# Hybrid conv/HGRN2/MoE layer on one core: the output half of a tile follows its own recurrence by two tiles instead of by a block of four

## What is computed

```python
h = rms_norm(x, g_pre_mix) * (1.0 + sc1) + sh1
cv, cg, q, f, i, g = jnp.split(h @ w_in, IN_SPLITS, axis=-1)
y_conv = conv_module(cv, cg, dw_kernel, dw_bias, conv_ln_gain, conv_ln_bias)  # GLU, 31 taps, LayerNorm, swish
y_rec = hgrn2(q, f, i, g, lb_table, rec_norm_gain)   # chunks of 64, 4 heads, per-head RMSNorm, output gate
y = jnp.concatenate([y_conv, y_rec], axis=-1) @ w_out
x = x + gt1 * rms_norm(y, g_post_mix)
h = rms_norm(x, g_pre_ffn) * (1.0 + sc2) + sh2       # router, then top-2 of 32 SwiGLU experts
x = x + gt2 * rms_norm(hier_moe(h, ...), g_post_ffn)
```

## Time and profile before

| | us |
|---|---|
| median of 3 runs | 1842.37 (1840.76 to 1842.48) |
| the profiled execution | 1839.05 |
| its span, first to last instruction | 1837.5 |
| `project` of blocks 1, 2, 3 | 135.3, 135.4, 135.5 |
| `steps` of blocks 0, 1, 2, 3 | 126.9, 127.2, 127.3, 120.1 |
| tail of the mixer | 75.0 |
| routing and experts | 626.9 |

### The profile page before, as it was taken

One profiled execution on the slowest core, in us unless ns is written; L12 is line 12 of the kernel. 1 busy time (PEld: TensorE's weight loads), 2 busy tenths in 40 slices (PEclk: granted clock), 3 DMA queues, 4 the chain that ended last, 5 costly groups with the idle time before them and its releaser, 6 DMA issues. The chain is left out here.

```text
span 1837.5 us, 24383 instructions
## 1 busy us (share of the span) xinstructions
PE 1533.9 (83%) x7268; PEld 1152.0 (63%) x7270; DVE 1296.4 (71%) x1999; ACT 841.1 (46%) x1443; POOL 374.0 (20%) x403
## 2 busy tenths in 40 slices
PE   2597945699998899998899998926989999999960
PEld 2486824488855789666689475425667666666730
DVE  5489966679965499865599652257667877778738
ACT  1422232433363522454322542313767787878745
POOL 1000000000010000010000010114546666665640
PEclk9999966799998899998899998956989999999985
DMA  9255114133322232322331122372999998889948
GB/s 341 76 157 187 52 43 163 64 94 107 98 81 71 81 110 73 92 92 92 84 100 47 38 89 81 126 237 82 314 338 301 302 341 263 241 229 315 279 97 363
DMA packets 200424, 291.29 MB, mean 159 GB/s; under 512 B 10558, under 2 KB 158171, under 8 KB 200346
## 3 DMA queue, kind: packets, MB, share of 16 engines
q1 hardware_dynamic: 169762, 193.03, 31.4%
q0 software_dynamic: 30416, 97.19, 18.9%
q10 hardware_dynamic: 168, 0.06, 0.0%
HBM read 240.42 MB, written 59.26 MB: 163 GB/s over the span
## 5 line engine op out<-in xcount | busy, mean ns | idle before, releaser
L892 DVE SCALAR_TENSOR_TENSOR cv<-u,taps,cv 128x512 f32<-128x512 f32 x480 | 321.7, 743 | 0.6 <-DVE yT L848 0.3
L1741 DVE TENSOR_TENSOR w_rest<-wgu,w_high 128x1024 fp32r<-128x1024 f32 x192 | 233.7, 1221 | 94.5 <-ACT w_high L1666 93.3
L1666 ACT ACTIVATE w_high<-wgu 128x1024 fp32r x192 | 201.5, 1054 | 139.3 <-PE pgu L1616 86.0
L416 PE MATMUL bank<-hT_high,tiles_operand 128*128 128x512 f32 x512 | 204.6, 400 | 35.7 <-DVE hT_operand L866 21.1
L417 PE MATMUL bank<-hT_operand,tiles_operand 128*128 128x512 f32 x512 | 203.2, 397 | 0.0
L418 PE MATMUL bank<-hT_high,win_operand 128*128 128x512 f32 x512 | 202.9, 396 | 0.0
L439 PE MATMUL bank<-wo,yT 128*128 128x512 f32 x432 | 189.7, 594 | 0.0
L1626 PE MATMUL py<-wd,hTe 128*128 x384 | 172.6, 592 | 0.9 <-ACT yb L1693 0.9
L1614 PE MATMUL pgu<-w_high,x_high 128*128 128x512 f32 x384 | 155.3, 404 | 0.0
L1616 PE MATMUL pgu<-w_high,x_rest 128*128 128x512 f32 x384 | 151.0, 393 | 0.0
L1615 PE MATMUL pgu<-w_rest,x_high 128*128 128x512 f32 x384 | 151.0, 393 | 0.0
(11 more groups left out here) (345 smaller groups left out, 2910.4 us busy)
## 6 DMA issues: line engine op xcount, KB each, us to landing
win<-w_in_in SPq DMA_DIRECT2D x64, 512.0 KB, 5.2
wgu<-w_gate_in SPq DMA_DIRECT2D x32, 1024.0 KB
wgu<-w_up_in SPq DMA_DIRECT2D x32, 1024.0 KB
wd<-w_down_in SPq DMA_DIRECT2D x32, 1024.0 KB
wo<-w_ada_in POOLq DMA_DIRECT2D x8, 2048.0 KB, 9.2
win<-w_in_in SPq DMA_DIRECT2D x16, 1024.0 KB, 5.2
y_dram<-zeros POOLq DMA_DIRECT2D x17, 512.0 KB, 5.3
win<-x_in SPq DMA_DIRECT2D x16, 512.0 KB, 4.5
```

What stands on the lines that cost most here:

```text
L416: nc.tensor.matmul(out[:], high[:, k, cols], hT_high[:, k, :], start=(k == 0), stop=False)
L892: ins = V.scalar_tensor_tensor(out=cv[:, j], in0=u[:, j, w:w + T], scalar=tap, in1=cv[:, j], op0=ALU.mult, op1=ALU.add)
L1666: A(w_high[:, QK * q:QK * q + QK, :], c.wgu[:, bass.ds(slot, 1), QK * q:QK * q + QK, :].rearrange("p a k n -> p (a k) n"), ACT.Copy).then_ ...
L1741: V.tensor_tensor(w_rest[:, part, :], c.wgu[:, bass.ds(slot, 1), part, :].rearrange("p a k n -> p (a k) n"), w_high[:, part, :].bitcast(F3 ...
```

## The change

- The unit of delay is the tile. In `steps(t)` the output half is done for four tiles w = 0 to 3 that are numbers 4t-2+w (`tile_no`): the last two tiles of block t-1, and the **first two of block t itself**. Thus `steps(0)` gets two tiles of it, the steps of blocks 1 to 3 four each as before, and the tail has two instead of four.
- For that, a tile's outputs are normed, gated, turned and saved by themselves: `orstd` and `gateo` and `oT` for each i, in the order of the lists. The outputs of tiles 2 and 3 are turned in the next block's `project`, behind its first piece. `yT` holds two tiles instead of a block, so `place` copies one tile at a time, when the `y` two tiles before has been done.
- All three lists are new. TensorE turns the tiles of block t+1 (`T` 0, `T` 1) right behind `B` 1 and ahead of `O` 1; `T` 2 and `T` 3 ahead of `O` 3; the lists end with `O` 3, `r` 3, `l` 2 and `l` 3.
- `centre`, `sq` and the first `ysum` move into `heads`, between the heads' exponentials.
- `win_high` gets a third buffer, so a piece may be rounded when the piece three before has been used. The added slot is free memory for `xsum` and for two tiles of `last_modulation`.
- In block 0 the products of w_ada's fifth vector move from VectorE (`ada_sums(4)`) to TensorE (`ada_products(4)`, 64 matmuls with one column behind `mean`). Its pieces 10 and 11 can be loaded only behind those products, and w_out behind `ada_sums(5)`, which VectorE does at `scale` and `mask` 0. `last_modulation` comes behind `B` 1 on TensorE and `osave` 0 on VectorE instead of behind `O` 3.

```diff
-        tiles, win_high = overlaid("tiles", [P, 2, 2 * D])
+        tiles, win_high = overlaid("tiles", [P, NSLOT, 2 * D])
...
-        yT = sb("yT", [P, KD, T])
+        yT = sb("yT", [P, 2, KD, P])
...
-        STEPS = [("y", 0, 0), ("mean",), ("y", 0, 1), ("y", 1, 0), ("var",), ("A", 0), ("y", 1, 1), ("B", 0), ("r", 0), ("O", 0),
...
+        tile_no = lambda t, w: t * NT - 2 + w
+        STEPS = [("y", 0, 0), ("mean",), ("y", 0, 1), ("var",), ("y", 1, 0), ("A", 0), ("y", 1, 1), ("B", 0), ("r", 0), ("A", 1), ("O", 0),
+                 ("l", 0), ("B", 1), ("T", 0), ("T", 1), ("O", 1), ("r", 1), ("A", 2), ("oT", 0), ("l", 1),
+                 ("y", 2, 0), ("B", 2), ("y", 2, 1), ("oT", 1), ("O", 2), ("y", 3, 0), ("y", 3, 1),
+                 ("A", 3), ("r", 2), ("B", 3), ("T", 2), ("T", 3), ("O", 3), ("r", 3), ("l", 2), ("l", 3)]
+        TAIL = [("y", 0, 0), ("y", 0, 1), ("y", 1, 0), ("y", 1, 1), ("r", 0), ("l", 0), ("r", 1), ("l", 1)]
...
+                if not isinstance(t, int) or t < NB:
+                    wait_apart(pool, proj_ready, (t + 1) * AU, pool_passed)
...
+            store(0, (2, 3))
+            with pool.Fori(1, NB) as t:
+                store(t, (0, 1, 2, 3))
+            store(NB, (0, 1))
...
+            def ada_products(m):
+                for half in range(2):
+                    p = 2 * m + half
+                    pe.wait_ge(*ada_load(p))
+                    for j in range(KD):
+                        for k in range(4):
+                            last = nc.tensor.matmul(bank[3][:, m * KD + j:m * KD + j + 1], ada_slot[slot_of(p)][:, k, j * P:(j + 1) * P],
+                                                    cond[:, 4 * half + k:4 * half + k + 1], start=(half == 0 and j == 0 and k == 0),
+                                                    stop=(half == 1 and k == 3), skip_group_check=True)
+                    last.then_inc(ada_used, 1)
+                pe.wait_ge(ada_used, 2)
+                pe.sem_inc(ada_cols_done, 1)
             def ada_columns(m):
...
+                    if j == 0 and not with_ada:
+                        turn_outputs(t - 1, 2)
+                        turn_outputs(t - 1, 3)
+            def y_half(t, w, half, take):
+                if half == 0:
                     pe.wait_ge(wo_in, 16)
-                    pe.wait_ge(yT_rec, (t + 1) * NT)
-                    pe.wait_ge(yT_conv, (t + 1) * NCH)
-                out = next(banks)
+                    pe.wait_ge(yT_rec, tile_no(t, w) + 1)
+                    pe.wait_ge(yT_conv, tile_no(t, w) + 1)
+                out = take(("y", w, half))
                 for k in range(KD):
...
+                if i >= 2:
+                    pe.wait_ge(yT_rec, t * NT + i - 1)
...
             def turn_outputs(t, i):
+                pe.wait_ge(o_gated, t * NT + i + 1)
                 if i == 0:
-                    pe.wait_ge(o_gated, t + 1)
-                if i >= 2:
-                    pe.wait_ge(yT_rec, t * NT + i - 1)
+                    pe.wait_ge(keT_ready, t * NT + 3)
+                else:
+                    pe.wait_ge(state_ready, t * 2 * NT + (5 if i == 1 else 2 * NT))
...
+            steps(0, 2, True, {("mean",): lambda: ada_products(4), ("B", 1): last_modulation})
...
-                if j >= 2:
-                    act.wait_ge(proj_ready, t * AU + 2 * (j - 2) + 2)
-                elif before is not None and j == 0:
-                    act.wait_ge(logit_ready, (before + 1) * NT)
-                    for s in range(2):
-                        act.wait_ge(x1_stored[s], (before + 1) * 32)
-                        act.wait_ge(xn_stored[s], (before + 1) * 32)
-                A(win_high[:, j % 2], win[:, j % NSLOT], ACT.Copy).then_inc(high_ready, 1)
...
+                if j >= NSLOT:
+                    act.wait_ge(proj_ready, t * AU + 2 * (j - NSLOT) + 2)
+                elif isinstance(before, int) and before == 0 and j == 0:
+                    act.wait_ge(row_done, 2)
+                elif before is not None and j == 1:
+                    act.wait_ge(logit_ready, tile_no(before, 3) + 1)
+                    for s in x1_stored:
+                        act.wait_ge(s, 32 * before + 16)
+                elif before is not None and j == 2:
+                    for s in xn_stored:
+                        act.wait_ge(s, 32 * before + 16)
...
+                    if j == 0 and before is not None:
+                        save_turned(before, 2)
+                        save_turned(before, 3)
...
+                    if h == 0:
+                        squares(t)
...
+                    if h == 2 and first == 0:
+                        y_sums(t, 0, place_of(STEPS))
...
-            ORDER = [("sq",), ("ysum", 0), ("var",), ("key", 0), ("x1sum", 0), ("ysum", 1), ("rin", 0), ("osq", 0), ("key", 1),
...
+            ORDER = [("var",), ("x1sum", 0), ("key", 0), ("gate",), ("ysum", 1), ("rin", 0), ("key", 1), ("osq", 0), ("orstd", 0),
+                     ("x1sum", 1), ("xsum", 0), ("xsum", 1), ("osq", 1), ("orstd", 1), ("T", 0), ("T", 1), ("rin", 1),
+                     ("key", 2), ("turned", 0), ("xsum", 2), ("xsum", 3), ("ysum", 2), ("turned", 1), ("osq", 2), ("orstd", 2),
+                     ("x1sum", 2), ("key", 3), ("ysum", 3), ("rin", 2), ("T", 2), ("T", 3), ("split", 0), ("x1sum", 3),
+                     ("osq", 3), ("orstd", 3), ("rin", 3), ("split", 1)]
...
+                centre(t)
...
-            def gate_outputs(t):
-                dve.wait_ge(o_rstd, t + 1)
-                o3 = ob[:].rearrange("p i (h n) -> p (i h) n", h=NH)
-                V.tensor_tensor(o3, o3, sums[:, 32:48].unsqueeze(2).to_broadcast([P, NT * NH, P]), ALU.mult).then_inc(v_rec, 1)
-                dve.wait_ge(v_rec, t + 1)
-                dve.wait_ge(g_done, t + 1)
-                V.tensor_tensor(ob[:], ob[:], gs[:], ALU.mult).then_inc(o_gated, 1)
...
+            def gate_outputs(t, i):
+                dve.wait_ge(o_rstd, t * NT + i + 1)
+                for h in range(NH):
+                    hc = slice(h * P, (h + 1) * P)
+                    last = V.scalar_tensor_tensor(out=ob[:, i, hc], in0=ob[:, i, hc], scalar=sums[:, 32 + 4 * i + h:33 + 4 * i + h],
+                                                  in1=gs[:, i, hc], op0=ALU.mult, op1=ALU.mult)
...
-            ORDER = [("centre",), ("ynorm", 0), ("scale",), ("mask", 0), ("x1norm", 0), ("state", 0), ("ynorm", 1), ("osave", 0), ("oms", 0),
...
+            ORDER = [("ynorm", 0), ("scale",), ("mask", 0), ("x1norm", 0), ("state", 0), ("ynorm", 1), ("osave", 0), ("mask", 1), ("conv",),
+                     ("oms", 0), ("place", 0), ("x1norm", 1), ("state", 1), ("gateo", 0), ("logit", 0), ("xnorm", 0), ("xnorm", 1), ("osave", 1),
+                     ("T", 0), ("T", 1), ("oms", 1), ("mask", 2), ("logit", 1), ("gateo", 1), ("place", 1), ("input", 0), ("input", 1),
+                     ("state", 2), ("xnorm", 2), ("xnorm", 3), ("osave", 2), ("ynorm", 2), ("oms", 2), ("x1norm", 2), ("mask", 3), ("gateo", 2),
+                     ("ynorm", 3), ("state", 3), ("place", 2), ("T", 2), ("T", 3), ("input", 2), ("input", 3), ("osave", 3), ("x1norm", 3),
+                     ("piece", 0), ("oms", 3), ("logit", 2), ("gateo", 3), ("place", 3), ("logit", 3), ("piece", 1)]
...
+            steps(0, 2, True, {("scale",): lambda: ada_sums(5, (0,)), ("mask", 0): lambda: ada_sums(5, (1,)),
+                               ("osave", 0): last_modulation})
...
```

More of the change, by code:

```diff
@@ L1075, in steps @@
+            TAIL_ORDER = [("ynorm", 0), ("x1norm", 0), ("ynorm", 1), ("x1norm", 1), ("logit", 0), ("logit", 1)]
+            def steps(t, first, nxt, after={}):
+                places = place_of(STEPS)
+                for step in ORDER:
+                    kind, *at = step
                     if kind in ("ynorm", "x1norm", "logit"):
-                        if out:
+                        if at[0] >= first:
                             if kind == "x1norm":
-                                x1_norm(t - 1, *at)
+                                x1_norm(t, *at)
```

448 lines of the change are left out of this document (236 added, 212 removed), and 5 rows, old and new, of the table STEPS.

## The result

The changed kernel takes 1874.3 us (median of 4 runs, 1870.16 to 1878.05); the kernel before took 1841.98 beside it. The ratio is 1.0178 (95% interval 1.0157 to 1.0199): slower by 32 us, where 21 were forecast. The profiled execution took 1870.16 us for a span of 1868.6, which is 31.1 more than before.

A forecast was written before the change was run, and what follows sets the result against it. TensorE's idle time in the steps, set by the order of three lists, was taken as the bound. 27.7 + 27.4 - 0.7 - 33.4 = +21.0 on the median 1842.37 gave 1863 us; forecast 1847 to 1877, range with rival 3 1840 to 1884.

The forecast's parts named there:

- block 0, to `project(1)`: Block 0 with two tiles of output half inside: ends at 382.5 instead of 354.8, +27.7 us.
- two middle blocks: Steps of the two middle blocks: 140.9 us each against 127.2, 13.7 more, +27.4 us for both.
- last block and tail: From the last block's steps to the last matmul: 161.7 us against 195.1, -33.4 us.
- The layout by hand: Three engines' lists of a middle block laid out by durations from the rows: 33.4 us idle of 135.0.
- The price of half clock: Middle block: three restarts of TensorE at half clock add 6.5 us; bounds nothing (+9 in all) to double (+33).
- I take 17, since only their start runs at half clock: Block 0's 64 one-column products on TensorE: 17 us, between 14.7 and 28.6.
- I get 80: Block 0 from `T` 0 to its end: 80 us, where a middle block takes 77.8.
- The hidden edits: Third buffer, GpSimd's stores and residual loads, SyncE's `load_x` 2 and 3, `gateo` in four parts: counted at nothing.
- Rival 1: Block 0 takes its two tiles into its idle time: -13, 1829 us, faster; chance 0.12.
- Rival 2: TensorE is fed throughout; a middle block takes 105 us, tail -38: 1760 us; chance 0.04.
- Rival 3: TensorE at half clock between all waits in three blocks: +20, 1883 us; chance 0.12.
- Rival 4: The moves cancel by layout errors of a few us at each stop: within 0.2%; chance 0.05.

The follow-up runs named there:

- x6: Changed kernel with `x1sum` 3 ahead of `T` 2 on ScalarE and `x1norm` 3 ahead of `input` 2 on VectorE: 1860.98 us.
- x1: Changed kernel with both `xnorm` ahead of `conv` on VectorE and both `xsum` ahead of `osq` 0 on ScalarE: 1870.62 us.
- x4: Changed kernel's structure with all three lists reordered by the layout until hardly a stop was left: 1754.8 us, ratio 0.9533.
- x2: Changed kernel with `O` 1 ahead of `T` 0 and `T` 1 on TensorE: 1862.89 us.
- x10: Changed kernel with the fifth vector of w_ada summed by VectorE again and both halves of the sixth behind `state` 0: 1868.2 us.
- x5: Kernel before the change, its three lists alone reordered by the same layout: 1804.61 us, ratio 0.9806.
- x8: Changed kernel with 8 unused matmuls of 256 columns among block 0's 64 one-column products: 1876.67 us.
- x9: Changed kernel with the fifth vector of w_ada summed by VectorE again, ahead of `scale`, without the one-column products: 1877.16 us.

## Why the prediction was right, and where it was off

The direction and the mechanism held. The forecast was +21 in the span; the trace has +31.1. By the terms of the sum:

| | forecast | measured |
|---|---|---|
| block 0, to `project(1)` (354.80 to 386.24) | +27.7 | +31.4 |
| `project(1)` | -0.7 | +0.1 |
| two middle blocks (521.61 to 1073.14, before 490.09 to 1015.51) | +27.4 | +26.1 |
| last block and tail (1073.14 to 1237.92) | -33.4 | -30.3 |
| routing and experts | 0 | +3.8 |

**The middle blocks.** The layout by hand forecast waits of 11.0, 6.2, 2.9, 1.6, 0.9, 9.1 and 1.8 us; `steps(1)` has 10.90, 5.97, 0.78, 1.23, 0.76, 8.64 and none for `l` 3, and the long ones were ended by the instructions that were named. x6 shows that the last is ScalarE's `x1sum` 3. Of the first, x1 shows that the reason given (`xnorm` 0 behind `gateo` 0) was only the last of two: `logit` 0 stands there as well. The price of half clock was put equal in both blocks; the trace has 141.4 for `steps(1)` and 136.6 for `steps(2)` with the same lists, and 136.9 and 136.7 for the `project` behind them, 1.2 to 1.5 more than before, where 0.65 less was forecast. The sum came out within 1.3, but by luck in its parts. Two rows by windows, `steps(1)` and `steps(2)`:

```profile
521.61:662.96 141.35, 112.94 (x490) 73.64 (x489) 77.20 (x152) 70.04 (x156) 11.01 (x16) 0.85 0.32 97
799.90:936.50 136.60, 109.67 (x490) 71.74 (x489) 77.18 (x152) 69.99 (x155) 11.09 (x16) 0.87 0.33 101
```

The forecast for one of these stages was 33.4 us idle and 108.1 busy (101.6 and 6.5 for half clock). The first has 28.4 idle and 112.9 busy: the waits came out 5 us shorter, and half clock cost 5 us more than its term (x4, with the same work at a clock of 0.99, is busy for 101.2). The second has 26.9 and 109.7, and the `project` behind each was 2 us longer than forecast.

**Block 0: the mis-sized term.** "I take 17, since only their start runs at half clock" was wrong in size and in kind. The products took 22.27 us, and it is their end that runs at half clock. The windows of the changed kernel over the two parts of the stretch:

```profile
233.00:244.00 11.00, 11.00 (x76) 10.80 (x75) 9.75 (x13) 6.62 (x15) 0.74 (x1) 0.76 0.34 79
244.00:255.60 11.60, 11.47 (x54) 11.39 (x55) 7.53 (x13) 4.40 (x9) 0.00 (x0) 0.50 0.45 175
```

By it, and by `var` behind it (5.45 us for 3.45), `scale` ended at 265.0 instead of 258.5. `T` 0 started at 306.1 instead of 302: from `scale` to `state` 0 the layout had put 2.6 us too much, which hid a part. The stretch behind `T` 0 took 80.1 us, where "I get 80" stands. In other kernels, where nothing ahead of the products differs, they took 25.0 (x1, x2, x4), so the 22.3 are one trace's number. Both lie between the bounds that were given (14.7 and 28.6); `var` was done 6.3 us later than forecast (260.9 for 254.6), and 3.7 of them reached `project(1)`. x10 confirms the path itself by the time of each step.

**Last block and tail.** 164.8 us for 161.7. The steps took 119.7 for the 118.4 of the layout with its five us for half clock, the rest, from the two `oT` at 1192.88, 45.0 for 43.3. The end of the steps and the start of the tail show half clock:

```profile
1186.88 6.20 PE L486 MATMUL bank<-wroute,tiles 128*128 128x36 f32 x32
...
1194.80 8.62 PE L469 MATMUL pS<-wo,yT 128*128 128x512 f32 x16
```

At full clock these are 3.7 and 7.0, 4.1 us less. That this is the reason for the 3.1 is likely and not shown.

**Experts: a term that was not there.** From the first matmul of the experts (1296.33, before 1269.01) to the end are 572.3 us, before 568.5. The program is the same there, and TensorE is busy for 490.0 us and for 488.8. x5, in the old structure, has 568.2. Ten kernels in the new one have 572.0 to 574.2, but x8, in the new one too, has 569.1. So the lists don't decide it, and neither does the structure alone. The three kernels in which TensorE is busy there for less than 489 us are just the three with less than 570 (x8: 488.4), and the ten others are busy for 489.9 to 493.4. What does it is not known, and this stays open.

**The hidden edits.** The third buffer could take effect nowhere in `project`: ScalarE rounds piece j + 2 behind the halves of piece j, which it saves itself, so its list never lets it be three ahead. This is read from the code; no kernel ran without the buffer. `project(1)` took 135.4 us (before 135.3), as that has it.

**The rivals.** Rival 1 (block 0 takes its tiles into its idle time) did not happen here, and x4 shows that it can: `project(1)` at 358.07. Its reason against ("at the end of a chain") was a property of the lists and not of the structure. Rival 2 forecast 1760 us for a TensorE that is fed throughout; these lists don't feed it, and x4, whose lists do, took 1754.8. Rival 3 (half clock between all waits) has a share of the truth: of the 10 us that the forecast lacks, 3.7 come through the late `var`, behind products at half clock, and the 3.1 of the last block and tail lie beside half-clock rows. Its own sum was off: 7.6 us more in each of three blocks are 22.8 and not 20, so that it stood at 1886, just outside the range that was to take it in. Rival 4 (within 0.2%) is out by the interval of 1.0157 to 1.0199.

The Trainium skill, TensorE: Matmul & The Clock Gate, part 1, says that the array falls back to 1.2 GHz once it has stood idle. The trace agrees behind the waits of 10.90 and 8.64 us (3.67 us for two `T` that take 2.0 when warm, 6.88 for two `l` that take 3.7). Short waits differ: behind the same wait of 1.23 us `T` 2 and `T` 3 together took 2.19 us in `steps(1)` and 3.37 in `steps(2)`. The trace doesn't show why the clock fell in the one-column products, where the profile has TensorE busy for 22.27 of 22.3 us, and no run here found the reason.

## What to carry to other kernels

When work moves between queues that are served in order, lay out every engine's list by its durations and reorder by that layout: the restructuring that lost 32 us with one set of lists won 86 with another. A long wait in such a list is several waits deep, so take away its named releaser and look at what ends it then (x1 won 4 us at most, where the bracket showed 11 a block). Before moving work off an engine, see whether it fits a gap there, and what waits behind it where it goes (x9, x10).
